# Gated recurrence by products of gates over doubling blocks, in a two-layer hybrid transformer block

## The reference

```
log_f = log(fg);  bcum = cumsum(gj, axis=2)            # within a chunk
decay = exp(bcum[j] - bcum[i])  for i <= j
scores[j, i] = sum_k q[j, k] * decay[j, i, k] * k[i, k]
o = scores @ v + (q * exp(bcum)) @ state
new_state = exp(blast) * state + (k * exp(blast - bcum)).T @ v
```

## Time and profile before

| | us |
|---|---|
| median of 3 runs | 2141.57 (2140.95 to 2141.94) |
| profiled execution | 2142.22 |
| its span, first to last instruction | 2140.3 |
| mean granted TensorE clock | 0.981 |
| one steady iteration of the mixer's loop | 47.6 |

### The profile page before, as it was taken

The page is one execution under the profiler, slowest core; times in us unless marked ns, Lnnn a source line. Parts: engine busy times, 40 slices in busy tenths (PEclk is TensorE's granted clock), DMA queues, the critical chain, the costliest instruction groups (busy, mean ns, idle before and its releaser), DMA issues.

```text
span 2140.3 us, 28594 instructions
## 1 busy us (share of the span) xinstructions
PE 1992.0 (93%) x9946; PEld 1630.0 (76%) x9946; DVE 871.4 (41%) x1253; ACT 731.4 (34%) x1044; POOL 927.8 (43%) x455
## 2 busy tenths in 40 slices
PE   5999999888889899999979999998888889999997
PEld 4888888776658688888768888887666677888886
DVE  7322210587785622210172222017777855222102
ACT  4322222444543422232242223224444444222321
POOL 4444444343443444444344444444344334444452
PEclk9999999999999999999989999999999999999998
DMA  4322233121112222323213222322111113232331
GB/s 147 108 92 94 97 100 117 58 83 39 49 39 79 79 98 98 98 95 112 70 60 110 96 95 91 118 91 96 44 47 49 49 60 98 98 98 98 98 108 50
DMA packets 52041, 182.26 MB, mean 85 GB/s; under 512 B 6248, under 2 KB 7304, under 8 KB 51976
## 3 DMA queue, kind: packets, MB, share of 16 engines
q1 hardware_dynamic: 51976, 181.38, 25.6%
HBM read 178.87 MB, written 2.49 MB: 85 GB/s over the span
## 4 chain that ended last, share of the span: by engine, by line
PE 70%; DVE 11%; issue 8%; DVEq 4%; ACT 3%; POOL 2%; POOLq 1%; ACTq 1%; DMA 0%; SPq 0%
PE bank L667 22%; PE bank L669 22%; PE bank L668 22%; DVE QC L1080 2%; POOL WLO L350 2%; DVE HLO L924 1%; POOLq L375 1%; DVEq L1092 1%; PE bank L875 1%; DVE KZ L1081 1%; ACT HHI L446 1%; DVEq L948 1%; DVE SM L1097 1%; PE bank L877 1%; ACT WHI L429 1%
## 5 line engine op out<-in xcount | busy, mean ns | idle before, releaser
L350 POOL TENSOR_TENSOR WLO<-RAW,WHI 128x1024 fp32r<-128x1024 f32 (+1 forms) x336 | 801.8, 2405 | 1046.6 <-ACT WHI L429 1046.5
L667 PE MATMUL bank<-HHI,WHI 128*128 128x512 f32 (+1 forms) x2000 | 780.8, 390 | 67.3 <-POOL WLO L350 40.7
L668 PE MATMUL bank<-HLO,WHI 128*128 128x512 f32 (+1 forms) x2000 | 763.8, 382 | 0.0
L669 PE MATMUL bank<-HHI,WLO 128*128 128x512 f32 (+1 forms) x2000 | 763.1, 382 | 0.0
L667 PEld LDWEIGHTS bank<-HHI,WHI 128*128 128x128 f32 x2000 | 382.8, 191 | 151.9 <-POOL WLO L350 54.8
L669 PEld LDWEIGHTS bank<-HHI,WLO 128*128 128x128 f32 x2000 | 382.3, 191 | 71.9
L668 PEld LDWEIGHTS bank<-HLO,WHI 128*128 128x128 f32 x2000 | 383.2, 192 | 69.5 <-issue 1.7
L429 ACT ACTIVATE WHI<-RAW 128x1024 fp32r<-128x1024 f32 (+1 forms) x336 | 337.9, 1038 | 67.6 <-PE bank L669 66.9
L667 PE MATMUL bank<-UHI,WHI 128*128 128x512 f32 (+1 forms) x792 | 294.3, 372 | 0.0
L669 PE MATMUL bank<-UHI,WLO 128*128 128x512 f32 (+1 forms) x792 | 292.9, 370 | 0.0
L668 PE MATMUL bank<-ULO,WHI 128*128 128x512 f32 (+1 forms) x792 | 292.8, 370 | 0.0
(11 more groups left out here) (171 smaller groups left out, 1362.3 us busy)
## 6 DMA issues: line engine op xcount, KB each, us to landing
RAW<-stream SPq DMA_DIRECT2D x336, 512.0 KB, 3.3
X<-xT SPq DMA_DIRECT2D x4, 512.0 KB, 7.0
yT<-X SPq DMA_DIRECT2D x8, 256.0 KB, 2.0
rel_scratch<-KZ SPq DMA_DIRECT2D x1, 382.0 KB
mask_sb<-masks SPq DMA_DIRECT2D x1, 256.0 KB, 9.9
bias<-rel_scratch SPq DMA_DIRECT2D x2, 128.0 KB
par<-params SPq DMA_DIRECT2D x1, 60.0 KB, 2.4
par<-sinks SPq DMA_DIRECT2D x2, 2.0 KB, 3.5
```

Source lines behind the costliest of these rows:

```text
L350: pool.tensor_tensor(WLO[:, n, 0:cols], RAW[:, n, 0:cols], WHI[:, n, 0:cols], ALU.subtract)\
L667: pe.matmul(dst, WHI[:, slot, lhs], rhs_hi, start=first, stop=False)
L668: pe.matmul(dst, WHI[:, slot, lhs], rhs_lo, start=False, stop=False)
L669: ins = pe.matmul(dst, WLO[:, slot, lhs], rhs_hi, start=False, stop=last)
```

## The change

Logarithm, scan, exponents and exponentials go. The levels run upwards, m = 1, 2, 4, ... 64, and keys KE and queries QE are scaled in place. At level m, KE of a token already holds its key times the gates from behind it to the end of its block of m, and QE its query times the gates from its block's start; their product is the score for two neighbouring blocks. Then `widen` multiplies the lower block's keys by the upper block's total gate product, the upper block's queries by the lower block's, and a tree of products (TREE_F) gives the totals of the next size. After the last level KE and QE are the operands of the state update and of the state's output, so KH, QB and edec go too. The diagonal is a product of its own (`diagonal`).

Each level is now eight matmuls, one per chunk and head, with 64 key channels in the rows, 128 keys (64 in the last level), and the 64 queries of the upper halves as strided moving columns; their results lie in two-bank PSUM tensors (`pair`). Two levels are picked at a time, the last one is copied by ACT. The output product is in the order chunk, then head, first all masked scores, then all states. KE is rewritten only when the previous pair's key transposes are read.

The loop over t is unrolled on PE, DVE, ACT and POOL. The next pair's takes are spread over DVE's order (next_take), with gate and query preparation for pair t+1 (`inputs`, `keys`, ACT's `gates`) inside iteration t; for pair 0 they stand ahead of the loop, behind the copies of the attention's value windows on ACT. The projection order becomes F, Q, QA, I, the first pair's F and Q being computed with the keys and values of the attention. The lower clamp of the gate (FG_MIN) goes. Work of POOL in the loop: two weight splits, the sum of squares' addition, two weight splits.

```diff
-FG_MIN = 2.0 ** -63
-HALVES = [64, 32, 16, 8, 4, 2]
+HALVES = [1, 2, 4, 8, 16, 32, 64]
-STAGES = NLEV + 3
-F, QA, Q, I = range(4)
+STAGES = NLEV + 1
+NPICK = NLEV - 1
+PICKS = 1 + NPICK // 2
+LEVEL_PAIR = [1, 1, 1, 1, 0, 0, 1]
+TREE = [0]
+for _m in HALVES:
+    TREE.append(TREE[-1] + SEQ // (2 * _m))
+F, Q, QA, I = range(4)
...
+def gates(t):
     act.preload_act_table_set("sigmoid_and_others")
+    act.wait_ge(proj_free, L * LAYER_JOBS + (J_GROUP0 + 4 * t + F + 1 + PROJ_BANKS))
     act.activation(SIGF, PROJ[:, F, :], ACT.Sigmoid)
     act.activation(SIGNF, PROJ[:, F, :], ACT.Sigmoid, scale=-1.0)
+    act.wait_ge(proj_free, L * LAYER_JOBS + (J_GROUP0 + 4 * t + Q + 1 + PROJ_BANKS))
     act.activation(SIGQ, PROJ[:, Q, :], ACT.Sigmoid).then_inc(sig_ready, 1)
     act.preload_act_table_set("natural_log_exp_and_others")
+def head_norm(t):
+    act.wait_ge(yh_sum, L * NT + (t + 1))
+    rsqrt_mean(YR[:, t, :], bank[7][:], HEAD_DIM).then_inc(yh_r, 1)
+gates(0)
+for t in range(NT):
+    it = L * NT + t
+    def ahead(n):
+        split_hi(L, C_GROUPS + 4 * t + n + 2)
+    act.wait_ge(vtok_full, it + 1)
+    act.activation(VTOK[:].rearrange("p a b -> p (a b)"), bank[6][:], ACT.Copy).then_inc(vtok_ready, 1)
+    if t > 0:
+        head_norm(t - 1)
     act.wait_ge(logit_ready, it + 1)
     act.activation(S[:], S[:], ACT.Exp).then_inc(exp_ready, 1)
+    ahead(0)
     for half in range(2):
         act.wait_ge(pt_full, it * 2 + (half + 1))
         act.activation(PT[:, 4 * half:4 * half + 4, :].rearrange("p a b -> p (a b)"),
+                       bank[4 + half][:], ACT.Copy).then_inc(pt_ready, 1)
+    act.wait_ge(pv_full, it + 1)
+    act.wait_ge(sq_free, L * LAYER_SQ + (Q_YA + t + 2))
+    act.activation(SQ[:, 0, :], bank[4][:], ACT.Square).then_inc(sq_done, 1)
+    act.activation(Y[:, t, :], bank[4][:], ACT.Copy).then_inc(ya_ready, 1)
     ahead(1)
+    if t < NT - 1:
+        gates(t + 1)
+    ahead(2)
+    act.wait_ge(lv_used, it * PICKS + PICKS)
+    act.wait_ge(lv_full, it * (NLEV + 1) + (NLEV + 1))
+    act.activation(SM[0:P // 2, :, P // 2:],
+                   pair[LEVEL_PAIR[NLEV - 1]][0:P // 2, :].rearrange("p (n u q) -> p n u q", n=2 * HCHUNKS, u=2)[:, :, 0, :],
+                   ACT.Copy).then_inc(top_used, 1)
     act.wait_ge(kht_full, it + 1)
+    act.activation(KHT[:].rearrange("p a b -> p (a b)"), bank[4][:], ACT.Copy).then_inc(kht_ready, 1)
+    ahead(3)
     act.wait_ge(o_full, it + 1)
+    act.activation(Y[:, NT + t, :], bank[6][:], ACT.Copy)
     act.activation(YSQ[:], bank[6][:], ACT.Square).then_inc(yh_sq, 1)
+head_norm(NT - 1)
...
+def head_pairs(at, keys, moving):
     for c in range(HCHUNKS):
         for h in range(2):
             rows = slice(64 * h, 64 * h + 64)
+            ins = pe.matmul(at(h, c), KE[rows, c * P:c * P + keys], moving(rows, c), start=True, stop=True)
+    ins.then_inc(lv_full, 1)
+def diagonal():
+    pe.wait_ge(logit_read, it + 1)
+    pe.wait_ge(staged, it * STAGES + 1)
+    pe.sem_inc(held)
+    head_pairs(lambda h, c: pair[0][:, h * SEQ + c * P:h * SEQ + c * P + P], P,
+               lambda rows, c: PROJ[rows, Q, c * P:c * P + P])
+def scores(l):
+    m = HALVES[l]
+    if l == 0:
+        pe.wait_ge(vtok_ready, it + 1)
+        pe.wait_ge(yh_r, it + 1)
+    elif l == 2:
+        pe.wait_ge(lv_used, it * PICKS + 2)
+    elif l == 4:
+        pe.wait_ge(ya_ready, it + 1)
+    elif l == 6:
+        pe.wait_ge(lv_used, it * PICKS + 3)
+    pe.wait_ge(staged, it * STAGES + (l + 1))
+    pe.sem_inc(held)
+    keys = P // 2 if l == NLEV - 1 else P
+    def at(h, c):
+        first = h * SEQ + c * P + l % 2 * (P // 2)
+        return pair[LEVEL_PAIR[l]][0:keys, first:first + P // 2].rearrange("p (b m) -> p b m", m=m)
+    def moving(rows, c):
+        return QE[rows, t % 2, c * P:c * P + P].rearrange("p (b u m) -> p b u m", u=2, m=m)[:, :, 1, :]
+    head_pairs(at, keys, moving)
+pe.wait_ge(proj_free, L * LAYER_JOBS + (J_GROUP0 + 4 * t + QA + 1 + PROJ_BANKS))
 pe.sem_inc(held)
 for n in range(8):
     for h in range(2):
                         PROJ[rows, QA, CHUNK * n:CHUNK * n + CHUNK],
                         kT[rows, CHUNK * n:CHUNK * n + P], start=True, stop=True)
 ins.then_inc(qk_full, 1)
+if t > 0:
+    total(YSQ[:], 7, (yh_sq, it), yh_sum, block_ones)
+pe.wait_ge(proj_free, L * LAYER_JOBS + (J_GROUP0 + 4 * t + I + 1 + PROJ_BANKS))
+for c in range(HCHUNKS):
+    ins = pe.transpose(bank[6][:, c * P:c * P + P], PROJ[:, I, c * P:c * P + P], ident[:])
+ins.then_inc(vtok_full, 1)
+next_group(0)
+diagonal()
+scores(0)
+next_group(1, 0, 4)
 pe.wait_ge(p_ready, it + 1)
+pe.wait_ge(lv_used, it * PICKS + 1)
 pe.wait_ge(vwin_ready, L * 2 + 2)
 for n in range(8):
+    ins = pe.transpose(bank[4 + n // 4][:, (n % 4) * P:(n % 4) * P + P], Slog[:, n, :], ident[:])
     if n % 4 == 3:
         ins.then_inc(pt_full, 1)
...
+    scores(1)
+    next_group(1, 4, 7)
     pe.wait_ge(pt_ready, it * 2 + 2)
     for n in range(8):
         for h in range(2):
             ins = pe.matmul(bank[4][rows, CHUNK * n:CHUNK * n + CHUNK], vwin[:, n, rows],
                             PT[:, n, rows], start=True, stop=True)
     ins.then_inc(pv_full, 1)
+    scores(2)
+    next_group(1, 7, 8)
+    next_group(2, 0, 2)
+    scores(3)
+    next_group(2, 2, 5)
+    scores(4)
+    next_group(2, 5, 8)
+    scores(5)
+    next_group(3, 0, 2)
+    scores(6)
+    next_group(3, 2, 4)
+    pe.wait_ge(staged, it * STAGES + STAGES)
+    pe.wait_ge(lv_used, it * PICKS + PICKS)
     for c in range(HCHUNKS):
+        ins = pe.transpose(bank[4][:, c * P:c * P + P], KE[:, c * P:c * P + P], ident[:])
     ins.then_inc(kht_full, 1)
+    next_group(3, 4, 6)
     pe.wait_ge(kht_ready, it + 1)
     for c in range(HCHUNKS - 1):
         for h in range(2):
             rows = slice(64 * h, 64 * h + 64)
+            ins = pe.matmul(bank[5][rows, 64 * c:64 * c + 64], KHT[:, c, rows], VTOK[:, c, rows],
                             start=True, stop=True)
     ins.then_inc(ds_full, 1)
+    next_group(3, 6, 8)
+    pe.wait_ge(top_used, it + 1)
+    for c in range(HCHUNKS):
+        for h in range(2):
+            rows = slice(64 * h, 64 * h + 64)
+            pe.matmul(bank[6][rows, c * P:c * P + P], VTOK[:, c, rows], SM[:, h * HCHUNKS + c, :],
+                      start=c == 0, stop=False)
+    pe.wait_ge(st_ready, it + 1)
+    pe.sem_inc(held)
+    for c in range(1, HCHUNKS):
+        for h in range(2):
+            rows = slice(64 * h, 64 * h + 64)
+            ins = pe.matmul(bank[6][rows, c * P:c * P + P], ST[rows, c - 1, :], QE[rows, t % 2, c * P:c * P + P],
+                            start=False, stop=c == HCHUNKS - 1)
     ins.then_inc(o_full, 1)
+total(YSQ[:], 7, (yh_sq, L * NT + NT), yh_sum, block_ones)
 total(RP[:], 4, (sq_free, L * LAYER_SQ + (Q_YA + NT + SQ_SLOTS)), ya_sum)
...
+take(L, C_KV + 3, PROJ[:, F, :], bank[0][:], four=(1, 2)).then_inc(proj_free, 1)
+take(L, C_KV + 3, PROJ[:, Q, :], bank[1][:]).then_inc(proj_free, 1)
...
-for buf in (KZ, QC, SM):
-    dve.memset(buf[:], 0.0)
+dve.memset(SM[:], 0.0)
 dve.memset(RP[:], 0.0)
+def inputs(t):
+    dve.wait_ge(sig_ready, L * NT + (t + 1))
+    dve.tensor_scalar(FG, SIGF, lb[:, NT + t:NT + t + 1], lb[:, t:t + 1], ALU.mult, ALU.add)
+    dve.tensor_tensor(PROJ[:, Q, :], PROJ[:, Q, :], SIGQ, ALU.mult)
+    dve.drain()
+    pairs = FG.rearrange("p (b u) -> p b u", u=2)
+    dve.tensor_tensor(TREE_F[:, 0:TREE[1]], pairs[:, :, 0], pairs[:, :, 1], ALU.mult)
+    dve.tensor_tensor(QE[:, t % 2, :], PROJ[:, Q, :], FG, ALU.mult)
+def keys(t):
+    if t > 0:
+        dve.wait_ge(kht_full, L * NT + t)
+    dve.tensor_scalar(KE[:], SIGNF, lb[:, NT + t:NT + t + 1], None, ALU.mult).then_inc(staged, 1)
+inputs(0)
+keys(0)
+for n in (QA, I):
+    take(L, C_GROUP0 + n, PROJ[:, n, :], bank[n][:]).then_inc(proj_free, 1)
+for t in range(NT):
...
+next_take(0)
...
+def widen(l):
+    m, blocks = HALVES[l], SEQ // (2 * HALVES[l])
+    factor = (TREE_F[:, TREE[l - 1]:TREE[l]] if l > 0 else FG).rearrange("p (b u) -> p b u", u=2)
+    halves = lambda a: a.rearrange("p (b u m) -> p b u m", u=2, m=m)
+    lower, upper = halves(KE[:])[:, :, 0, :], halves(QE[:, t % 2, :])[:, :, 1, :]
+    dve.wait_ge(lv_full, it * (NLEV + 1) + (l + 2))
+    if l > 0:
+        dve.tensor_tensor(TREE_F[:, TREE[l]:TREE[l + 1]], factor[:, :, 0], factor[:, :, 1], ALU.mult)
+    dve.tensor_tensor(lower, lower, factor[:, :, 1:2].to_broadcast([P, blocks, m]), ALU.mult)
+    dve.tensor_tensor(upper, upper, factor[:, :, 0:1].to_broadcast([P, blocks, m]), ALU.mult)\
+        .then_inc(staged, 1)
+def pick(l):
+    m = HALVES[l]
+    mask = mask_sb[:, 64 * l:64 * l + 64].rearrange("p (b m) -> p b m", m=m)
+    src = pair[LEVEL_PAIR[l]][:].rearrange("p (n u b m) -> p n u b m", n=2 * HCHUNKS, u=2, m=m)[:, :, l % 2]
+    dve.drain()
+    dst = SM[:].rearrange("p n (b u m) -> p n b u m", u=2, m=m)[:, :, :, 1, :]
+    return dve.copy_predicated(dst, mask.unsqueeze(1).to_broadcast([P, 2 * HCHUNKS, 64 // m, m]), src)
```

(73 more changed lines are left out.)

269 lines of the change are left out of this document (37 added, 232 removed).

## The result

The changed kernel takes 2120.51 us (median of 4 runs, 2120.22 to 2121.16) against 2141.26 for the kernel before on the same chip: ratio 0.9903, 95% interval 0.9891 to 0.9916. It is faster by 20.8 us where 44.6 were forecast. Its profiled execution took 2120.33 us, with a span of 2118.2.

The account below looks back on a forecast made before the run. PE work plus DVE hand-offs bound the loop. Period 38.4 + 0.8 = 39.2 us; per layer 7.3 + 2.5 + 4 x 39.2 - 0.9 = 165.7 against 188.0; twice the 22.3 gain gives 2097 us, range 2078 to 2128.

Parts of the forecast that it names:

- The tail: Behind the loop's last output products, 628.06 to 635.19: keeps its chain of squares, sum, rsqrts and scaling, so no change.
- The output products: Masked-score by value and state by query matmuls, now alternating halves: 1.7 us against 4.77, a gain of 3.1 per iteration.
- The entry: Before each layer's first QK^T: PE idle 7.3 us until 447.4, plus 2.5 us for half clock behind it.
- Rival D: Weight loads bind the score levels: 1.7 us for six, 0.85 for the last, +5.1 per iteration, 2138 us; chance 0.04.
- Rival A: Score levels at the lower bound, 0.55 us each: period some 37.6 us, time 2084; chance 0.15.
- C: PE waits for a widen at each level, POOL's 11 us come on top: 2185 us; 0.05 with other ways above 2146.
- Rival B: DVE hand-offs late: a two-SBUF-operand product beside POOL's split loses 2.1 us; period 41.3, time 2114; chance 0.22.
- Step one: PE's score levels: 0.9 us for six and 0.55 for the last, 5.95 against 5.0, a loss of 0.95 per iteration.
- Step two: DVE's widens, 0.8 to 0.9 us, fit behind PE's work between score levels; picks take 0.8 to 0.95.
- Rival E: Strided operands at half rate on DVE: +0.7 us per widen, +0.8 per pick, mostly hidden; 2105; chance 0.52 with the forecast.
- Step three: POOL's splits cost PE time only at the diagonal copy or widens 5 and 6, 2.1 us for one hit.
- Step four: PE's restarts around stalls: seven cost 1.1 us beside their brackets; with one or two left, about 0.8 is saved.

Follow-up runs that it names:

- experiment 4: Changed kernel with the output products back in the old order, masked-score and state product in turn: 2145.89 us, ratio 1.0019 to the kernel before.
- experiment 3: Changed kernel with the last score level computed for all 128 keys instead of 64: 2123.87 us, ratio 0.9916 to the kernel before.
- experiment 5: Changed kernel with the first two levels' masked copies in blocks of 4 instead of 1 and 2: 2116.55 us, ratio 0.9888 to the kernel before.
- Experiment 2: Changed kernel with ACT copying an iteration's first two weight tiles one step earlier, so POOL's splits move: 2111.23 us, ratio 0.9858 to the kernel before.
- experiment 9: Changed kernel with earlier entry queries and gates, earlier weight copies, one K-tile before scores(2), and the last pair's weight copy later: 2086.50 us, ratio 0.9742.
- experiment 6: Changed kernel with one K-tile moved from behind scores(2) to before it: 2125.64 us, ratio 0.9927 to the kernel before.
- experiment 7: Changed kernel with earlier ACT weight copies and one K-tile moved before scores(2): 2111.06 us, ratio 0.986 to the kernel before.
- experiment 8: Changed kernel with earlier entry queries and gates, earlier ACT weight copies, and one K-tile before scores(2): 2093.19 us, ratio 0.9776 to the kernel before.

## Why the prediction was wrong

The direction was right. The time lies in the stated range, but the gain came out at less than half of the forecast. Nearly all that was missed lies in the four iterations: they take 43.32, 41.69, 41.85 and 42.41 us, together 169.3, where 2.5 + 4 x 39.2 - 0.9 = 158.4 was forecast. That is 10.9 in layer 0, and twice that is 21.8 of the 22.7 us that are missing in the profiled execution. The tail, which was to stay, adds 0.5 per layer (7.64 from the last output product to the next K-tile, 7.13 before): PE waits 1.18 us there for ACT's square, which a K-tile covered before.

**Right.** The output products: 1.7 forecast, 1.73 measured, confirmed by experiment 4. The entry: QK^T at 447.4 forecast, 447.43 measured. Iteration 0 is 2.6 us longer than a steady one less its sum of squares, against 2.5; that the two agree so well is luck, since about 2.2 of it is the slow clock and 0.4 a wait at the softmax transposes. The widens 5 and 6 were hidden, there is no wait at the key transposes, and the output products and the next QK^T wait for nothing. Rival D is out: a level has 16 loads in 1.04 us, 65 ns each. The Trainium skill ("TensorE: Matmul & The Clock Gate", LDWEIGHTS) has 107 ns for a load; halves that alternate don't pay that here. Rival A is out as well. So is C in its size: one widen in an iteration makes PE wait for POOL, two in a layer's last pair. Rival B's figures, 41.3 for the period and 2114, came closest to the measured 41.69 and 2120.5, but partly by luck: its one hit was priced at 2.1 us and costs 1.0 to 1.3, and the rest has other causes.

**Step one that failed: the levels.** "I take 0.9 for six levels and 0.55 for the last": measured 0.94 to 1.04 and 0.61, 6.73 together against 5.95, so +0.8. The value lay between the bounds 0.55 and 1.09; it belonged at the end with the same stationary side, as experiment 3 shows.

**Step two: "The widen fits behind each"**, with picks at "0.8 to 0.95". That was the mean of four copies, 3.79 us in all. The fourth of them alone takes 1.31, the other three 0.73: the row by form of L1097 in the kernel before has it.

```profile
L1097 DVE COPY_PREDICATED SM<-mask_sb,bank x48: 709/725/1315, 469.8 to 1680.8; 128x512 f32<-128x512 uint32 x40, 64x512 f32<-64x512 uint32 x8
```

Rival E had priced such a copy at 0.8 us more, which is near. Its sentence "L1081 and L1097 show none down to blocks of 2" against it was misread for the copies. It was right for the products: the widens take 0.42 at every block. The new kernel has two copies at 1.31, levels 0 and 1, and they come first, where the walk had given the wait to the diagonal's copy. They cost the 0.67 at scores(2): with copies of 0.72 in experiment 5 that wait is gone.

**Step three: the place of the collision.** Rival B's mechanism was the right one, but I let it decide only at "the close places (diagonal copy, widens 5 and 6)". It struck widen(2), behind the late copies, for 1.0 us and no more, since the rest of the 2.2 us lay beside K-tiles, and in a layer's last pair widen(3) as well, for 0.83. The walk gave DVE its own durations and never laid POOL's splits beside them, though ACT's place in its queue fixes when they start. Experiment 2 moves them and gets it back. The Trainium skill ("SBUF — State Buffer", two separate sides) has a DVE instruction with two SBUF inputs and a GpSimd one shut each other out for a whole instruction; the 2.62 us beside a split of 2.40 agree.

**Step four: the time saved around the stalls.** The forecast had 38.4 us of work for PE in an iteration. The steady iteration of experiment 9 has no wait, so its 39.89 us are all PE's work, 1.5 more. The levels are 0.8 of that. About 0.4 more is "Seven stalls, 1.1 us; with one or two left, about 0.8 is saved". The forecast put 0.16 us beside each bracket, from 502.72 to 504.10 less 1.22. But the last matmul of a K-tile and a small matmul behind it start 0.32 us apart (499.25 to 499.57) instead of 0.23 without any wait, so some 0.07 of the 0.16 goes with the stall. The periods say the same: 41.69 less 39.89 is 1.80, for waits of 0.67 and 0.99. The last 0.3 isn't assigned to a row.

**The sum.** A steady period is 2.5 us over the forecast: 1.5 of work, of which the levels are 0.8; and 1.8 for the two waits, where 0.8 was charged for one at the softmax transposes, so 1.0. The waits are thus the smaller part of the miss, but the part that could be had by order alone: experiments 2 and 6 together (experiment 7) take the whole 1.8 out. 2086.50 lies 10.5 us below the forecast in spite of the added work, since the forecast's own 0.8 went too and the entry, which it had priced nearly right, was mended as well.

**Open.** Why the runs of experiment 5 scatter over 7.6 us. Why the clock falls behind one wait of 1.68 us and not behind the next, and behind 1.18 us in experiment 4 and not in the changed kernel. Whether a pick of level 0 between the two first levels would shorten DVE's chain: PE would write into the bank that DVE reads, and no run has it.

## What to carry to other kernels

When a chain alternates between two engines, walk it with each instruction's own duration, taken by form and not as a mean over a group, and lay the instructions of the third engine that shares SBUF with them beside it: an engine with 12 us to spare in 42 still made PE wait twice. Before a K-tile is moved to cover a wait, ask what the waiting engine's next hand-off is; a wait that only moves and merges with another can cost more than both. Don't count as saved with a stall what every change from large to small matmuls costs anyway. A new dependency at a loop's entry is paid once per layer, in full and with a slow clock behind it (8.8 us here): see first whether the first item can be asked for earlier in the other engines' queues.

## What the runs showed of the hardware

- A masked copy of 512 columns from PSUM takes 0.72 us, but 1.31 when its elements stand alone or in pairs (blocks of 1 and 2), in the kernel before (blocks of 2) and in the changed one (1 and 2). With blocks of 4 in their place (experiment 5) all copies took 0.70 to 0.73. Products of two SBUF operands with the same blocks stay at 0.42.
- For eight small matmuls on alternating row halves the stationary columns set the time: 1.04 us with 128 stationary and 64 moving, 0.99 with 128 and 128, 0.61 with 64 and 64.
- Beside a POOL instruction of 2.4 us a DVE product with two SBUF inputs took 2.62 us instead of 0.42, and one of 16 columns 2.04 instead of 0.17.
- In the profiles of experiments 6 to 8 there are twelve waits of PE of 1.67 or 1.68 us in the levels. Behind six of them the granted clock of the next stretch (1.5 to 6 us behind the restart) was 0.62 to 0.73, which means some of it at 1.2 GHz, behind the other six 1.00. Behind the split waits of 0.67 and 0.99 with a level and K-tiles between, behind those of 1.10 and 1.12, and behind one of 2.18, it was 1.00. But length alone doesn't decide it: behind the eight waits of 1.61 us at L799 in the kernel before it was 1.00, and behind the 1.18 us at the end of the loop it was 1.00 in the changed kernel and 0.62 and 0.61 in experiment 4, where slower output products (4.42 us instead of 1.73) stand before it. So such a wait can cost 1.5 us beside itself, and for those twelve did so half the time.
